# The low part of each weight tile on GpSimd: four instructions of 256 columns instead of one of 1024

## The reference

```
u = rmsnorm(h, g_pre_mix)
qa, ka, va, qb, kb, vb, qc, kc, vc = split(u @ w_in)          # 1024 x 3840
ya = diff_attention(qa, ka, va, ...)       # A: 4 heads, two maps each, causal by chunks of 64
yb = sliding_window_sink_attention(...)    # B: 8 heads, window of 2 chunks, a sink
yc = chunk_band_attention(qc, kc, vc, ...) # C: 8 heads, 8 chunks back
gates = sigmoid(u @ w_gate + b_gate)
mixed = gates[0]*(ya @ w_proj_a) + gates[1]*(yb @ w_proj_b) + gates[2]*(yc @ w_proj_c)
h = h + rmsnorm(mixed @ w_out, g_post_mix)
u = rmsnorm(h, g_pre_ffn)
h = h + rmsnorm((gelu(conv_gate(u @ w_up)) * conv_up(u @ w_up)) @ w_down, g_post_ffn)
```

## Time and profile before

| what | value |
|---|---|
| time, median of 3 runs | 913.95 us (913.28 to 915.84) |
| the profiled execution: time, span | 914.02 us, 912.2 us |
| TensorE (PE) busy | 877.4 us, 96% |
| VectorE (DVE) busy | 456.2 us, 50% |
| ScalarE (ACT) busy | 396.8 us, 43% |
| GpSimd (POOL) busy | 370.4 us, 41% |
| GpSimd, two L523 back to back, from 24.62 us | 4.70 us |
| mixing: from one unit's L1127 to the next (416.87 to 435.91 us) | 19.04 us |
| feed-forward: from one L523 to the next (609 to 614 us) | 5.44 us |
| granted TensorE clock, mean | 0.993; half in two short stretches of the first 30 us |

### The profile page before, as it was taken

The page is one execution under the profiler, slowest core; times in us unless marked ns, Lnnn a source line. Parts: engine busy times, 40 slices in busy tenths (PEclk is TensorE's granted clock), DMA queues, the critical chain, the costliest instruction groups (busy, mean ns, idle before and its releaser), DMA issues.

```text
span 912.2 us, 12771 instructions
## 1 busy us (share of the span) xinstructions
PE 877.4 (96%) x4327; PEld 739.3 (81%) x4327; DVE 456.2 (50%) x889; ACT 396.8 (43%) x700; POOL 370.4 (41%) x196
## 2 busy tenths in 40 slices
PE   6989889999999999999999999999999999999997
PEld 6877777888888887888887889888888888888886
DVE  5588887666665563333443075555555555400004
ACT  4465555666565554323333345444444334321112
POOL 4243223332232234555454553544444444444441
PEclk9899999999999999999999999999999999999999
DMA  7441133322122221423333612433333332322202
GB/s 230 127 115 47 47 92 92 91 69 76 52 71 58 82 70 43 131 83 101 103 102 120 220 53 88 121 92 92 92 98 108 93 92 92 130 101 93 93 24 92
DMA packets 132140, 86.13 MB, mean 94 GB/s; under 512 B 6822, under 2 KB 121454, under 8 KB 132098
## 3 DMA queue, kind: packets, MB, share of 16 engines
q1 hardware_dynamic: 131050, 81.86, 30.0%
q10 hardware_dynamic: 1048, 3.72, 1.1%
HBM read 83.42 MB, written 2.14 MB: 94 GB/s over the span
## 4 chain that ended last, share of the span: by engine, by line
PE 81%; DVE 12%; ACT 3%; issue 2%; DMA 1%; POOL 0%; DVEq 0%; SPq 0%; POOLq 0%; ACTq 0%
PE banks L1233 25%; PE banks L1235 25%; PE banks L1234 25%; PE banks L1377 2%; DVE scratch L1062 1%; DVE scratch L1033 1%; DVE pages L955 1%; DVE lam_ratio L1058 1%; DVE scratch L1069 1%; PE banks L1252 1%; PE banks L1306 1%; PE banks L1307 1%; DVE pages L975 1%; DMA wide<-in_g_pre_mix_dram 1%; DVE pages L996 1%
## 5 line engine op out<-in xcount | busy, mean ns | idle before, releaser
L523 POOL TENSOR_TENSOR ring_lo<-ring_raw,ring_hi 128x1024 fp32r<-128x1024 f32 x142 | 344.1, 2425 | 485.2 <-ACT ring_hi L626 485.0
L1233 PE MATMUL banks<-u_hi,ring_hi 128*128 128x512 f32 (+1 forms) x800 | 310.8, 388 | 0.6 <-DVE u_lo L895 0.6
L1235 PE MATMUL banks<-u_hi,ring_lo 128*128 128x512 f32 (+1 forms) x800 | 306.1, 383 | 0.0
L1234 PE MATMUL banks<-u_lo,ring_hi 128*128 128x512 f32 (+1 forms) x800 | 305.6, 382 | 0.0
L626 ACT CAST ring_hi<-ring_raw 128x1024 fp32r<-128x1024 f32 x142 | 147.7, 1043 | 132.5 <-PE banks L1235 125.2
L1235 PEld LDWEIGHTS banks<-u_hi,ring_lo 128*128 128x128 f32 x800 | 151.5, 189 | 29.5
L1233 PEld LDWEIGHTS banks<-u_hi,ring_hi 128*128 128x128 f32 x800 | 151.6, 190 | 28.1 <-DVE u_lo L895 0.9
L1234 PEld LDWEIGHTS banks<-u_lo,ring_hi 128*128 128x128 f32 x800 | 151.7, 190 | 27.2
L1198 DVE SCALAR_TENSOR_TENSOR wide<-banks,cols,wide 128x511 f32<-128x511 f32 x88 | 65.9, 749 | 87.4 <-ACT wide L848 80.6
L1233 PE MATMUL banks<-ring_hi,pages 128*128 128x512 f32 x240 | 93.8, 391 | 1.7 <-DVE scratch L1131 1.6
L1234 PE MATMUL banks<-ring_lo,pages 128*128 128x512 f32 x240 | 93.4, 389 | 0.0
(11 more groups left out here) (137 smaller groups left out, 1050.5 us busy)
## 6 DMA issues: line engine op xcount, KB each, us to landing
ring_raw<-in_w_ffn_up_dram SPq DMA_DIRECT2D x88, 256.0 KB, 3.1
ring_raw<-in_w_in_dram SPq DMA_DIRECT2D x60, 256.0 KB, 3.3
ring_raw<-in_w_gate_dram SPq DMA_DIRECT2D x48, 256.0 KB, 3.1
ring_raw<-in_w_ffn_down_dram SPq DMA_DIRECT2D x44, 256.0 KB, 2.7
ring_raw<-in_w_out_dram SPq DMA_DIRECT2D x16, 256.0 KB, 2.8
scratch<-in_x_dram SPq DMA_DIRECT2D x4, 512.0 KB, 6.3
ring_raw<-in_w_proj_a_dram SPq DMA_DIRECT2D x8, 256.0 KB, 2.8
ring_raw<-in_w_proj_c_dram SPq DMA_DIRECT2D x8, 256.0 KB, 3.1
```

Of the source, the lines that this page charges most:

```text
L523: pool.tensor_tensor(wlo[:, r, :], raw[:, r, :], whi[:, r, :].bitcast(F32), ALU.subtract).then_inc(w_lo_done, 1)
L1233: pe.matmul(out, lhs_hi, rhs_hi, start=start, stop=False)
L1234: pe.matmul(out, lhs_hi, rhs_lo, start=False, stop=False)
L1235: return pe.matmul(out, lhs_lo, rhs_hi, start=False, stop=stop)
```

## The change

`w_lo` issues four subtractions of 256 columns each instead of one of 1024. The wait for the high part stays ahead of the first, the signal `w_lo_done` stays on the last. `w_lo_early` is as before.

```
+LO_PIECES = 4
...
             def w_lo(t, r):
 
                 pool.wait_ge(w_hi_done, t + 1)
-                pool.tensor_tensor(wlo[:, r, :], raw[:, r, :], whi[:, r, :].bitcast(F32),
-                                   ALU.subtract).then_inc(w_lo_done, 1)
+                for i in range(LO_PIECES):
+                    c = slice(1024 // LO_PIECES * i, 1024 // LO_PIECES * (i + 1))
+                    last = pool.tensor_tensor(wlo[:, r, c], raw[:, r, c], whi[:, r, c].bitcast(F32), ALU.subtract)
+                last.then_inc(w_lo_done, 1)
```

## The result

The changed kernel takes 900.52 us (median of 4 runs, 900.42 to 900.81) where the kernel before takes 913.75 in the same comparison: a ratio of 0.9856, 95% interval 0.9842 to 0.987, or 13.2 us less. A second comparison gave 0.9849 (0.9825 to 0.9874). The forecast was 903.2, range 899 to 911.

The account below looks back on a forecast made before the run. TensorE's waits for VectorE, held up by whole 2.4 us GpSimd instructions, were taken as the bound. Terms 5.5 + 0.1 + 1.8 + 1.0 + 0.4 + 1.6 + 0.4 = 10.8 us, from 914.0 to 903.2; range 899 to 911.

Parts of the forecast that it names:

- A piece: Length of one 256-column GpSimd subtraction: taken as 0.70 us, between 0.59 and 1.01, so a tile takes 2.8 us.
- the power: GpSimd's dearest one-column instruction, L538, 0.55 us; taken as fixed part it set the upper bound of 1.01 us per piece.
- VectorE gets in between: Between two GpSimd pieces the waiting VectorE instruction is let in, so it waits for at most one piece.
- the rival without gaps: Four pieces hold the ports as one, VectorE waits 2.8 us instead of 2.4: 6.0 us slower, 920.0; chance 0.10.
- Branch A: Attention: TensorE's waits for L1062 shrink by 5.5 us plus 0.1 for a fifth, those for L1102 by 1.8.
- L1037's 0.27: Branch A: L1037 gets through 0.27 us earlier, at 86.50 instead of 86.77, and the later steps hang on it.
- Branch C and B: Attention: C's three waits go, 1.0 us; B gains 0.14 three times, 0.4, as each L1069 meets a new piece.
- Mixing: Last mixing unit: L1127 and L1131 end earlier and TensorE's whole wait of 1.6 us goes.
- Before the feed-forward part: L889 wins about 1.1 us, but low parts of tiles 2 and 3 end up to 2 us later: counted 0.
- First tiles: Start: L889 ends earlier but delays tile 1's low part, which TensorE needs next: gain 0.4 of 2.1 us.
- No wait of TensorE is for GpSimd: Whole kernel: GpSimd idles for 485 us and its low parts are ready tiles ahead, so TensorE never waits for it.

Follow-up runs that it names:

- start4: Kernel before with only the low parts of the first four tiles in four pieces, all others whole: 912.53 us against 914.25, ratio 0.998.
- mix4: Kernel before with only the mixing and output-product tiles in four pieces: 912.18 us, ratio 0.998.
- ffn4: Kernel before with only the tiles from the third of the feed-forward part on in four pieces: 914.03 us, ratio 0.9992.
- two512: Changed kernel with two pieces of 512 columns per tile instead of four: 909.26 us, ratio 0.9941 to the kernel before.
- clock_fill: Kernel before, whole instructions, plus 16 unit-matrix turns on TensorE in its early idle time: 913.63 us against 913.12, ratio 0.9999.
- eight128: Changed kernel with eight pieces of 128 columns per tile instead of four: 901.21 us, ratio 0.9858 to the kernel before.

## Why the prediction was right

*A piece.* Forecast 0.70 us, a tile 2.8; measured 2.82. The one-column arithmetic instruction was the right neighbour, not the power. The estimate that I drew from the Trainium skill (GPSIMD Engine Reference, "Elementwise — side-by-side cycle accounting"), 0.83, was too high: these runs give a fixed part of (2.82 - 2.40)/3 = 0.14 us, from which 128 columns come to 0.42, and 3.39/8 = 0.42 was measured.

*VectorE gets in between.* Right, and the rival without gaps is out: L1062 at 0.23. That four pieces carry no semaphore among them made no difference. The Trainium skill's rule (SBUF — State Buffer, "Who interferes with whom") of a pair held for one whole instruction agrees at every length tried: L1066 waited out one piece of 0.70 and one of 1.26.

*Branch A.* Forecast 1.45 for L1062 and 0.6 for L1102, 2.05 for a unit. Measured from one L1062 wait to the next: 26.79 us before (92.57 to 119.36), 24.74 after (85.78 to 110.52), 2.05. The chain L1037 first, L1058 second, L1062 third was needed for this: without L1037's 0.27 the sum would not close. Over the whole of branch A, up to its last long wait (at 146.16 and 135.26 us), 7.8 us were gained where 5.5 + 0.1 + 1.8 = 7.4 had been forecast.

*Branch C and B.* C kept 0.35 of 1.1. B was forecast at 0.4 and gave 0: the three long waits fell by 0.26 each, but the one at 250 us rose from 0.46 to 0.68 and one of 0.57 came new. Both are places where pieces make the tile longer and VectorE met its end; I had costed only the places where it already waited. From branch A's last long wait to the end of attention 1.1 us were gained, forecast 1.4. That attention as a whole came at 8.9 against 8.8 is in part luck: the misses in A and in B and C have opposite signs.

*Mixing.* 1.6 forecast, 1.65 measured.

*Before the feed-forward part.* Forecast 0 as a trade. The trade took place, waits for L889 2.0 to 0.8 and new ones for the low parts of tiles 2 and 3 of 0.2 and 0.65, and from the first of them to the end it came out at -0.5.

*First tiles.* This term was mis-sized: 0.4 forecast, 3.1 measured in the profiles. The trade of stalls was right: waits of 0.49 and 0.87 for one of 2.11, and TensorE goes on 0.3 us sooner. Some 0.9 is L917 and the VectorE steps behind it, which I had put at nothing because TensorE showed no wait there; it showed none because its own clock was at half. The other 1.9 is the half-clock stretch, which I had kept out of the sum and only in the range; that it was in the profile of before and not in that of after is chance in part, and no fixed part of the change. By median the start gave 1.7 us, with an interval from 0.3 to 3.3. Profile against profile the change gave 13.2 us where the steps forecast 10.8. Of the missing 2.4 the start alone is 2.7, and small losses elsewhere take 0.3 of it back.

*No wait of TensorE is for GpSimd.* Not quite: in the kernel before it stands 1.5 us for the unit matrix that GpSimd makes at the start (L516). No low part is waited for, so the sum does not change.

What stays open: why the half-clock stretch near 22 us comes only in some executions, and in these profiles only with whole instructions at the start. The filled idle time brought no measurable gain, which speaks against the shorter idle time of TensorE near 20 us as the cause, and few profiles of each kind don't settle it.

## What to carry to other kernels

An engine that nobody waits for can still set the time by making another one stand. Look for VectorE instructions whose duration ends with a GpSimd instruction's end, and ask of each whether TensorE waits behind it. Then first move the GpSimd work behind the step on the path, which cost one wait on a semaphore and gained 14.1 us here (12.1 of them in attention's trace), and only then cut it: pieces bound the stay, each adds its fixed part (0.14 us), and a chain of n such VectorE steps meets n pieces, as in branch B. Look too behind a stretch in which the engine on the path is slow for another reason: what stands there shows no wait, and costs once that reason is gone.

## What the runs showed of the hardware

GpSimd and VectorE take turns at instruction boundaries: a short VectorE instruction that comes while a piece runs goes before the next piece (L1062 of 0.23 us, L1066 of 1.19 in the changed kernel), and the next piece is recorded but stands (that tile took 3.26 us, an undisturbed one 2.83).

The granted clock fell inside attention too, after TensorE waits of 1.6 to 1.9 us, and only in some executions: the profiles of start4, mix4, ffn4 and two512, all with such waits, have between one and three half-clock stretches there; those of the kernel before and of clock_fill, with the same waits, have none, and neither has any kernel whose longest wait in attention is about 1.1 us. An execution's time goes with its mean granted clock: the kernel before took 911.92 us at 0.997 and 916.87 at 0.987 in one comparison, two512 906.29 at 0.996 and 912.09 at 0.989. The kernel before ranged over 911.6 to 918.2 us in all, start4, mix4, ffn4 and two512 over 4.1 to 6.5 us (without the execution of 1777 us), clock_fill over 2.7, and the kernels with attention treated over 0.4 to 3.1. That the waits make the clock fall is likely from this, but no run here varied them alone.

The trace of eight128 shows a granted clock of 0.95 where the others have 1.00, from start to end, with matmuls spaced as in the others; its three other executions are at 0.995 to 0.996 and take the same time. This is not explained.
